# Second feed-forward GEMM of a transformer block by one level of Strassen, two u tiles at a time

## The chip, the cores and the metric

One core of a Trainium2 chip. The metric is the device time of one execution in microseconds (us). Two times are told apart by this kernel's measurement where they differ by over 0.2%.

## What is computed

The reference is a residual block on x of 1024 rows (tokens) by 1024 columns, all float32: a combined projection, two attentions, gates and an output projection, and then the feed-forward part, the only one that is touched here:

```python
h2 = rms_norm(x, g_mlp[l])
x = x + jnp.square(jax.nn.relu(h2 @ w_ff1[l])) @ w_ff2[l]
```

with w_ff1 of 1024 x 4096 and w_ff2 of 4096 x 1024. Below, u is the squared relu, kept transposed: 32 tiles of 128 of its 4096 columns, each 128 partitions x 1024 tokens.

## The kernel before

**Numbers.** Every float32 operand is split into a high part, rounded to fp32r by a copy, and a low part, the difference (`split` L794 on POOL for weights, line L796 for the high and L798 for the low part; ACT and DVE for activations). A product is three matmuls: high by high, high by low, low by high (`split_products` L1267, whose one line L1273 issues all of these matmuls). A matmul has 128 x 128 stationary numbers and streams 512 columns.

**Stages.** Up to the feed-forward part (start to about 735 us) nothing is changed. There h2 stands transposed and split in mT_hi and mT_lo (also called h2T), and the residual x in xr, 8 tiles of 128 tokens x 1024.

**Feed-forward part.** It runs in FF_GROUPS = 8 groups of GROUP = 4 u tiles. For each u tile PE does 48 matmuls (`up_half` L1582: 8 contraction tiles, 3 passes, 2 halves of the tokens) into PSUM banks 0 to 3, two tiles taking turns. Behind the four tiles it does the second GEMM of the same group (`ff` L1602): for each of 8 token tiles 24 matmuls (4 u tiles, 3 passes, 2 halves of the output columns) that sum in PSUM banks 4 to 7, two token tiles taking turns. So a group is 192 + 192 matmuls. ACT (`ff_up` L1240) evacuates relu (L1247) and writes the square twice, once as float32 (L1254) and once rounded (L1261). DVE (`ff_vec` L1988) makes the low part (L1995) and adds each finished token tile to xr (L2001).

**What sets the order.** There is no scheduler: each engine has its own list of instructions, in the order of the code, and waits for counts of semaphores that others raise. POOL (`ff_splits` L972) splits a raw 128 x 1024 piece of weights for w1 or w2 at a time. SP (`ff_loads` L758) issues the loads of those pieces in a ring of two. The weights of the next group's first two tiles are split while PE is in the second GEMM or at its end. The stage in PE's list:

```python
for j in range(2 if first else 0, GROUP):
    pe.wait_ge(relu_ready, 8 * g + 2 * j - 2)
    up_half(g, j, (0, 1)).then_inc(up_done, 1)
for t in range(T):
```

Of the kernel before, what the change touches and what calls it, by code (L numbers as in the profile page):

```python
# [84 lines left out]
def build(nc, x, positions, g_mix, w_in, b_gate, g_qa, g_ka, sinks_a, g_cq, g_ckv,  # L85
# [6 lines left out]
    with ExitStack() as ctx:  # L92
# [269 lines left out]
        relu_ready = sem("relu_ready")
        relu_sq_ready = sem("relu_sq_ready")
        uT_hi_done = sem("uT_hi_done")
        uT_ready = sem("uT_ready")
# [183 lines left out]


# [6 lines left out]
        def _(sp):  # L557
# [200 lines left out]
            def ff_loads(g, first):  # L758
                def load(n, what, j, *split):
                    for s_, v in split:  # L760
                        sp.wait_ge(s_, v)
                    if what == 1:
                        src = w1_d[:, bass.ds(g * (GROUP * P) + j * P, P)].rearrange("(k p) n -> p k n", p=P)
                        dst = raw[n % 2][:, :].rearrange("p (k n) -> p k n", n=P)
                    else:
                        src = w2_d[bass.ds(g * (GROUP * P) + j * P, P), :]
                        dst = raw[n % 2][:, :]
                    sp.dma_start(dst, src).then_inc(raw_landed[n % 2], 16)
                load(0, 1, 0, (ow_ready, 7) if first else (w1_ready, 4 * g))
                load(1, 1, 1, (ow_ready, 8) if first else (w2_ready, 4 * g))  # L770
                load(2, 2, 0, (w1_ready, 4 * g + 1))
                load(3, 2, 1, (w1_ready, 4 * g + 2))
                load(4, 1, 2, (w2_ready, 4 * g + 1))
                load(5, 2, 2, (w2_ready, 4 * g + 2))
                load(6, 1, 3, (w1_ready, 4 * g + 3))
                load(7, 2, 3, (w2_ready, 4 * g + 3))
# [8 lines left out]
        def _(pool):  # L785
# [186 lines left out]
            def ff_splits(g, first):  # L972
                landed = 16 * 4 + 64 * g

                def unit(n, what, j):
                    pool.wait_ge(raw_landed[n % 2], landed + 16 * (n // 2 + 1))
                    if what == 1:
                        if first and j < 2:
                            pool.wait_ge(branch_done, 2 * KD)
                        else:  # L980
                            pool.wait_ge(up_done, 4 * g + j - 1)
                        split(raw[n % 2][:, :].rearrange("p (k n) -> p k n", n=P), w1_hi[j % 2][:, :, :],
                              w1_lo[j % 2][:, :, :], w1_hi_done, 4 * g + j + 1, w1_ready)
                    else:
                        if j == 0:
                            if first:
                                pool.wait_ge(x2T_done, 2 * KD)
                            else:
                                pool.wait_ge(down_done, T * g)
                        split(raw[n % 2][:, :], w2_hi[j][:, :], w2_lo[j][:, :], w2_hi_done, 4 * g + j + 1, w2_ready)  # L990
                unit(0, 1, 0)
                if first:
                    for t in range(T):
                        pool.wait_ge(x2_ms_ready, t + 1)
                        power(x_rstd[:, t:t + 1], x_ms[:, t:t + 1], 1, (P, 1)).then_inc(x2_rstd_ready, 1)
                unit(1, 1, 1)
                unit(2, 2, 0)
                unit(3, 2, 1)
                unit(4, 1, 2)
                unit(5, 2, 2)  # L1000
                unit(6, 1, 3)
                unit(7, 2, 3)
# [1021 lines left out]
```

## Time and profile before

| | |
|---|---|
| median of 3 runs | 1444.29 us (1444.26 to 1444.85) |
| the profiled execution, its own time | 1444.09 us |
| its span, first to last instruction | 1442.3 us |
| feed-forward part, first matmul to end of span | 734.85 to 1442.3 us |
| PE, DVE, ACT, POOL busy over the span | 98%, 37%, 26%, 36% |

The profile is of one execution. PE is the matmul engine, DVE the vector engine, ACT the activation engine, POOL the general one, SP the one that issues DMAs. Matmuls are pipelined, so that the busy time of one (389 ns) is longer than the distance from the start of one to the start of the next. In rows of the timeline "x24" means that many merged, and what stands in brackets is the idle time before them and who ended it.

### The profile page before, as it was taken

The page shows a single profiled execution, that of the slowest core. Times are in us where ns is not written, and L with a number is a line of the kernel's source. Part 1 is how long each engine was busy: PE and PEld are TensorE (multiplying, and loading weights), DVE is VectorE, ACT ScalarE, POOL GpSimd, SP SyncE. Part 2 cuts the span into 40 slices and gives each one's busy share as a digit, 9 for nine tenths or more (in the row PEclk, how much of TensorE's full clock was granted, in tenths as well). Part 3 has the DMA queues.
Part 4 walks back from the last instruction along what each step waited for, and adds up shares of the span by engine and source line. Part 5 has one row for each costly group of instructions (what it writes and reads, how often), then busy time and mean ns, then how long its engine had stood idle before and what let it go on. Part 6 is the DMA issues. An engine that isn't in the chain of part 4 may idle for free.

```text
span 1442.3 us, 17282 instructions
## 1 busy us (share of the span) xinstructions
PE 1409.5 (98%) x6792; PEld 1154.7 (80%) x6792; DVE 533.2 (37%) x947; ACT 367.8 (26%) x811; POOL 525.0 (36%) x381
## 2 busy tenths in 40 slices
PE   6999999999999999999999999999999999999998
PEld 6998776778877667888888888888888888888887
DVE  5402714533668762472443222222222213222222
ACT  5113235642456552010232020110301102021020
POOL 2332823436382610454045060431506125061420
PEclk9999999999999999999999999999999999999999
DMA  7120221211120015535012030110202102020102
GB/s 234 35 59 31 72 88 59 67 57 42 39 47 12 12 16 129 186 132 182 0 44 88 0 103 15 59 58 18 84 15 73 44 29 87 0 87 29 44 29 102
DMA packets 98105, 90.45 MB, mean 63 GB/s; under 512 B 21376, under 2 KB 84352, under 8 KB 98048
## 3 DMA queue, kind: packets, MB, share of 16 engines
q1 hardware_dynamic: 97904, 89.17, 20.4%
q8 instruction: 36, 0.59, 0.2%
q10 hardware_dynamic: 144, 0.52, 0.1%
q14 instruction: 21, 0.17, 0.0%
HBM read 76.99 MB, written 12.62 MB: 62 GB/s over the span
## 4 chain that ended last, share of the span: by engine, by line
PE 87%; DVE 5%; POOL 2%; ACT 2%; issue 2%; DMA 1%; ACTq 0%; DVEq 0%; SPq 0%; POOLq 0%
PE PS L1273 75%; PE PS L1467 3%; PE PS L1280 2%; PE PS L1366 1%; PE PS L1417 1%; DVE uT_lo L1995 1%; PE PS L1447 1%; PE PS L1388 1%; PE PS L1448 1%; PE PS L1368 1%; PE PS L1449 1%; PE PS L1431 1%; PE PS L1403 1%; ACT gate L1073 1%; POOL scA L914 0%
## 5 line engine op out<-in xcount | busy, mean ns | idle before, releaser
L796 POOL TENSOR_SCALAR w_hi<-raw 128x1024 fp32r<-128x1024 f32 x64 | 74.3, 1160 | 408.2 <-PE PS L1273 406.7
L1995 DVE TENSOR_TENSOR uT_lo<-relu_sq,uT_hi 128x512 fp32r<-128x512 f32 x64 | 92.0, 1472 | 279.0 <-ACT uT_hi L1261 279.0
L1247 ACT ACTIVATE relu_t<-PS 128x512 f32<-128x512 f32 x64 | 34.8, 595 | 553.3 <-PE PS L1273 553.3
L2001 DVE TENSOR_TENSOR xr<-PS,xr 128x1024 f32<-128x1024 f32 x64 | 78.4, 1224 | 245.7 <-PE PS L1273 245.7
L798 POOL TENSOR_TENSOR w_lo<-raw,w_hi 128x1024 fp32r<-128x1024 f32 x64 | 159.4, 2491 | 5.3
L1273 PE MATMUL PS<-mT_hi,w_hi 128*128 128x512 f32 x512 | 160.4, 389 | 0.7 <-POOL w_lo L798 0.7
L1273 PE MATMUL PS<-mT_hi,w_lo 128*128 128x512 f32 x512 | 160.3, 389 | 0.0
L1273 PE MATMUL PS<-mT_lo,w_hi 128*128 128x512 f32 x512 | 160.2, 389 | 0.0
L1273 PE MATMUL PS<-w_hi,uT_hi 128*128 128x512 f32 x512 | 158.4, 391 | 1.7 <-DVE uT_lo L1995 1.7
L1273 PE MATMUL PS<-w_lo,uT_hi 128*128 128x512 f32 x512 | 157.7, 389 | 0.0
L1273 PE MATMUL PS<-w_hi,uT_lo 128*128 128x512 f32 x512 | 157.7, 389 | 0.0
L1273 PEld LDWEIGHTS PS<-w_hi,uT_hi 128*128 128x128 f32 x512 | 95.6, 188 | 24.1 <-DVE uT_lo L1995 3.9
L1273 PEld LDWEIGHTS PS<-mT_hi,w_hi 128*128 128x128 f32 x512 | 96.1, 188 | 20.8 <-issue 0.9
L1273 PEld LDWEIGHTS PS<-w_hi,uT_lo 128*128 128x128 f32 x512 | 96.1, 188 | 20.0
L1273 PEld LDWEIGHTS PS<-w_lo,uT_hi 128*128 128x128 f32 x512 | 96.1, 188 | 20.0
L1273 PEld LDWEIGHTS PS<-mT_hi,w_lo 128*128 128x128 f32 x512 | 96.1, 188 | 20.0
L1273 PEld LDWEIGHTS PS<-mT_lo,w_hi 128*128 128x128 f32 x512 | 96.1, 188 | 19.9
L1273 PE MATMUL PS<-hT_hi,gw_hi 128*128 128x512 f32 x256 | 84.7, 412 | 5.0 <-ACT gate L1073 2.6
L1273 PE MATMUL PS<-hT_lo,gw_hi 128*128 128x512 f32 x256 | 79.4, 391 | 0.0
L1273 PE MATMUL PS<-hT_hi,gw_lo 128*128 128x512 f32 x256 | 79.2, 390 | 0.0
L1273 PE MATMUL PS<-zw_hi,hT_hi 128*128 128x320 f32 (+1 forms) x256 | 77.7, 303 | 0.0
L1273 PE MATMUL PS<-zw_hi,hT_lo 128*128 128x320 f32 (+1 forms) x256 | 77.0, 301 | 0.0
(208 smaller groups left out, 2390.0 us busy)
## 6 DMA issues: line engine op xcount, KB each, us to landing
raw<-in_w_ff SPq DMA_DIRECT2D x64, 512.0 KB, 3.7
g_raw<-in_w_in SPq DMA_DIRECT2D x16, 512.0 KB, 3.9
gate_store<-gate SPq DMA_DIRECT2D x16, 512.0 KB, 2.6
x_in<-in_x SPq DMA_DIRECT2D x8, 512.0 KB, 10.7
gate_a<-gate_store SPq DMA_DIRECT2D x8, 512.0 KB, 7.7
gate_b<-gate_store SPq DMA_DIRECT2D x8, 512.0 KB, 5.6
raw<-in_w_out SPq DMA_DIRECT2D x8, 512.0 KB, 3.6
xr<-in_x SPq DMA_DIRECT2D x8, 512.0 KB, 7.0
```

The costliest lines, as they stand in the source:

```text
L796: pool.tensor_scalar(hi_ap, raw_ap, 1.0, 1.0, ALU.mult, ALU.mult).then_inc(hi_done, 1)
L798: pool.tensor_tensor(lo_ap, raw_ap, hi_ap, ALU.subtract).then_inc(ready, 1)
L1073: act.activation(gate[u % 2][:, :], pair(gate_pair(u)), ACT.Sigmoid, bias=b_gate_c[:, u:u + 1]).then_inc(gate_ready, 1)
L1247: act.activation(relu_t[:, cols], PS[:, 2 * (j % 2) + h, :], ACT.Relu).then_inc(relu_ready, 1)
L1273: ins = pe.matmul(o, st, cut(mv), start=first and n == 0, stop=last and n == 2)
L1280: ins = pe.transpose(PS[0:rows, bank, i * P:(i + 1) * P], ap, ident[:, :])
L1366: pe.matmul(PS[:, bank, 0:B_GROUP * QK], cqT[:, c, rows], wuq[g % 2][:, c, :], start=c == 0, stop=c == 1)
L1368: pe.matmul(PS[:, bank, B_GROUP * QK:B_GROUP * (QK + P)], ckvT[:, rows], wukv[g % 2][:, :], start=True, stop=True).then_inc(proj_done, 1)
L1388: ins = pe.matmul(PS[:, 2 * s + g % 2, 256 * (g // 2):256 * (g // 2) + WIN], qaT[r:r + A_DIM, head // 2, m * P:(m + 1) * P], kaT[r:r + A_D ...
L1467: ins = pe.matmul(out[:, c0:HALF], vB[g % 3][:, kt, h % B_GROUP, :], p_tile(t)[:, c0:HALF], start=kt == 0, stop=last)
L1995: dve.tensor_tensor(uT_lo[:, j, cols], relu_sq[:, cols], uT_hi[:, j, cols], ALU.subtract).then_inc(uT_ready, 1)
L2001: dve.tensor_tensor(xr[:, t, :], pair(4 + 2 * (t % 2)), xr[:, t, :], ALU.add).then_inc(x3_added, 1)
```

## The change

The u tiles are taken in 16 pairs: pair i holds the tiles i and i + 16. The 2 x 2 blocks of a pair's product are: 512 tokens by one u tile on one side, one u tile by 512 output columns on the other. One level of Strassen (in Winograd's form) takes 7 products of such blocks instead of 8, out of sums and differences of the blocks. For a pair, PE does 7 products x 4 token tiles x 3 passes = 84 matmuls, each product into its own sum: four of them lie in the quarters of xr, three in sum1, sum6 and sum7 in SBUF. A product's token tile is 3 matmuls in one PSUM bank and is added to its sum at once by DVE. The last pair is done plainly (96 matmuls), while the running sums are folded into one another. The first GEMM keeps its 96 matmuls for a pair.

What the engines do for one pair i of the first 15: PE, `up` of pair i + 1 (2 tiles of 48 matmuls), then `down` of pair i (28 steps of 3). POOL: two splits of w1 (128 x 1024), 4 differences of w2 blocks and 7 splits of 128 x 512. ACT: 15 operations of 128 x 512. DVE: 4 sums and 7 low parts of 128 x 512, and 28 additions of a PSUM bank into a sum. A raw weight block is loaded into the place where later its low part stands (w2_raw, w1_raw), so that a load waits until PE has done with what was there. The loops of the stage are written out, in place of loops that run on the chip.

```diff
-GROUP = 4
-FF_GROUPS = D_FF // P // GROUP
+PAIRS = D_FF // P // 2
+BLOCKS7 = 28
+LAST = PAIRS - 1
...
-        uT_hi = place("uT_hi", 72, [P, GROUP, S], F32R)
-        uT_lo = place("uT_lo", 88, [P, GROUP, S], F32R)
-        relu_t = place("relu_t", 197, [P, S])
-        relu_sq = place("relu_sq", 201, [P, S])
+        w1_hi = [place(f"w1_hi{i}", 136 + 8 * i, [P, KD, P], F32R) for i in range(2)]
+        w1_lo = [place(f"w1_lo{i}", 140 + 8 * i, [P, KD, P], F32R) for i in range(2)]
+        w2_hi = [place(f"w2_hi{b}", 72 + 4 * b, [P, HALF], F32R) for b in range(7)]
+        w2_lo = [place(f"w2_lo{b}", 74 + 4 * b, [P, HALF], F32R) for b in range(7)]
+        u_hi = [place(f"u_hi{b}", 100 + 4 * b, [P, HALF], F32R) for b in range(7)]
+        u_lo = [place(f"u_lo{b}", 102 + 4 * b, [P, HALF], F32R) for b in range(7)]
...
+        sum1 = place("sum1", 128, [P, 4, HALF])
+        sum6 = place("sum6", 153, [P, 4, HALF])
+        sum7 = place("sum7", 193, [P, 4, HALF])
+        relu_t = place("relu_t", 201, [P, HALF])
+        r11 = place("r11", 203, [P, HALF])
+        r12 = place("r12", 205, [P, HALF])
...
+        PRODUCTS = (1, 2, 3, 5, 7, 6, 4)
+        AT = {p: b for b, p in enumerate(PRODUCTS)}
...
+        def wait_used(eng, i, p):
+            if i:
+                eng.wait_ge(down_done, BLOCKS7 * (i - 1) + 4 * AT[p] + 4)
+        def acc(p):
+            if p in (1, 6, 7):
+                return {1: sum1, 6: sum6, 7: sum7}[p][:, :, :]
+            rows, cols = {2: (0, 0), 3: (0, 1), 4: (1, 0), 5: (1, 1)}[p]
+            return xr[:, 4 * rows:4 * rows + 4, HALF * cols:HALF * cols + HALF]
...
+            def w1_load(i, j):
+                if i:
+                    sp.wait_ge(up_done, 2 * i - 1 + j)
+                f = i + PAIRS * j
+                sp.dma_start(w1_raw[j][:, :, :], w1_d[:, f * P:(f + 1) * P].rearrange("(k p) n -> p k n", p=P)
+                             ).then_inc(w1_landed[j], 16)
+            def w2_load(i, n):
+                p, row, col = ((1, 0, 0), (2, 1, 0), (3, 1, 1), (5, 0, 1))[n]
+                if i == 0:
+                    sp.wait_ge(o_done, 2 * T)
+                wait_used(sp, i, p)
+                f = i + PAIRS * row
+                sp.dma_start(w2_raw[AT[p]][:, :], w2_d[f * P:(f + 1) * P, HALF * col:HALF * col + HALF]
+                             ).then_inc(w2_landed[n], 16)
...
+            w1_load(1, 0)
+            for i in range(1, PAIRS):
+                w1_load(i, 1)
+                for n in range(3):
+                    w2_load(i, n)
+                if i + 1 < PAIRS:
+                    w1_load(i + 1, 0)
+                w2_load(i, 3)
...
+            def w1_split(i, j):
+                pool.wait_ge(w1_landed[j], 16 * (i + 1))
+                split(w1_raw[j][:, :, :], w1_hi[j][:, :, :], w1_lo[j][:, :, :], w1_hi_done, 2 * i + j + 1, w1_ready)
...
+            def w2_difference(out, a, b):
+                pool.tensor_tensor(w2_raw[AT[out]][:, :], w2_raw[AT[a]][:, :], w2_raw[AT[b]][:, :], ALU.subtract
+                                   ).then_inc(w2_step, 1)
+            def w2_first(i):
+                for n in range(4):
+                    if n != 1:
+                        pool.wait_ge(w2_landed[n], 16 * (i + 1))
+                wait_used(pool, i, 7)
+                w2_difference(7, 3, 5)
+                pool.wait_ge(w2_step, w2_count(i, "t3"))
+                w2_difference(5, 5, 1)
+                w2_high(AT[1])
+                w2_low(i, AT[1], "b11_hi")
+                wait_used(pool, i, 6)
+                w2_difference(6, 3, 5)
+                w2_high(AT[3])
+                w2_low(i, AT[3], "b22_hi")
+                w2_high(AT[5])
+                w2_low(i, AT[5], "t1_hi")
+            def w2_second(i):
+                pool.wait_ge(w2_landed[1], 16 * (i + 1))
+                wait_used(pool, i, 4)
+                if i == 0:
+                    pool.wait_ge(x2T_done, 2 * KD)
+                w2_difference(4, 2, 6)
+                w2_high(AT[2])
+                w2_low(i, AT[2], "b21_hi")
+                w2_high(AT[7])
+                w2_low(i, AT[7], "t3_hi")
+                w2_high(AT[6])
+                w2_low(i, AT[6], "t2_hi")
+                w2_high(AT[4])
+                w2_low(i, AT[4], "t4_hi")
...
+            def fold(into, p, blocks):
+                pool.wait_ge(acc_done, BLOCKS7 * (LAST - 1) + blocks)
+                pool.tensor_tensor(acc(into), acc(into), acc(p), ALU.add).then_inc(folded, 1)
+            w1_split(0, 0)
+            w1_split(0, 1)
+            for t in range(T):
+                pool.wait_ge(x2_ms_ready, t + 1)
+                power(x_rstd[:, t:t + 1], x_ms[:, t:t + 1], 1, (P, 1)).then_inc(x2_rstd_ready, 1)
+            w2_first(0)
+            w1_split(1, 0)
+            for i in range(LAST):
+                w2_second(i)
+                w1_split(i + 1, 1)
+                if i + 2 < PAIRS:
+                    w1_split(i + 2, 0)
+                if i + 1 < LAST:
+                    w2_first(i + 1)
+            fold(6, 1, 4)
+            fold(2, 1, 8)
+            w2_plain(0, 1, "b11_hi")
+            w2_plain(1, 2, "b21_hi")
+            w2_plain(2, 3, "b22_hi")
+            fold(3, 5, 16)
+            w2_plain(3, 5, "b12_hi")
+            pool.wait_ge(folded, 3)
+            fold(3, 6, 24)
...
+            def up(i, c):
+                j, k = c // KD, c % KD
+                if k == 0:
+                    pe.wait_ge(w1_ready, 2 * i + j + 1)
+                    pe.wait_ge(u_act, act_count(i - 1, ("relu21", "relu22")[j]))
+                ins = up_chunk(j, k, (0, 1))
+                if k == KD - 1:
+                    ins.then_inc(up_done, 1)
+            def down(d, n):
+                b, q = n // 4, n % 4
+                p, rows = PRODUCTS[b], slice(q * P, (q + 1) * P)
+                if q == 0:
+                    pe.wait_ge(u_vec, vec_count(d, U_OF[p]))
+                    pe.wait_ge(w2_step, w2_count(d, W_OF[p]))
+                if BLOCKS7 * d + n >= 4:
+                    pe.wait_ge(acc_done, BLOCKS7 * d + n - 3)
+                split_products(u_hi[b][:, rows], u_lo[b][:, rows], w2_hi[b][:, :], w2_lo[b][:, :],
+                               [(PS[:, 4 + q, :], whole)], 0, True, True).then_inc(down_done, 1)
...
+            for d in range(LAST):
+                for c in range(2 * KD):
+                    up(d + 1, c)
+                for n in range(BLOCKS7):
+                    down(d, n)
+            for t, k in ((0, 0), (1, 0), (0, 1), (1, 1)):
+                plain(t, k)
+            for t in range(2, T):
+                for k in range(2):
+                    plain(t, k)
...
+            def accumulate(d, n):
+                p, q = PRODUCTS[n // 4], n % 4
+                dve.wait_ge(down_done, BLOCKS7 * d + n + 1)
+                if q == 0 and d:
+                    dve.wait_ge(acc_done, BLOCKS7 * (d - 1) + n + 4)
+                if d == LAST - 1 and n == 4 * AT[6]:
+                    dve.wait_ge(folded, 1)
+                out, part = acc(p)[:, q, :], PS[:, 4 + q, :]
+                if d == 0 and p in (1, 6, 7):
+                    dve.tensor_copy(out, part).then_inc(acc_done, 1)
+                else:
+                    dve.tensor_tensor(out, part, out, ALU.add).then_inc(acc_done, 1)
...
+            def combine(d):
+                low(d, 2, r12[:, :], "hi12")
+                s2(d)
+                s4(d)
+                s1(d)
+                sum_low(d, 3, "s4_hi")
+                sum_low(d, 5, "s1_hi")
+                sum_low(d, 7, "s3_hi")
+                sum_low(d, 6, "s2_hi")
+                sum_low(d, 4, "hi22")
...
+            for d in range(LAST):
+                combine(d)
+                for n in range(BLOCKS7):
+                    accumulate(d, n)
+                low(d + 1, 1, r11[:, :], "hi11")
+                if d + 1 < LAST:
+                    s3(d + 1)
+                else:
+                    sum_low(LAST, 5, "hi21")
...
```

In the parts that are left out, `w2_high` and `w2_low` are the two halves of `split` for a block of w2, `act_count`, `vec_count` and `w2_count` give a step's number in the lists of ACT, DVE and POOL, `combine` and the ACT steps name blocks by 11, 12, 21, 22 (token half, u tile of the pair), and `plain` is the last pair.

POOL, the steps of one pair in the middle of the stage. Before, two tiles of w1 and then w2 pieces in turn, with one wait for PE at the start (w1_hi0 needs up_done), here from the first split of a group:

```order
L796 TENSOR_SCALAR w1_hi0<-raw0 128x1024 [waits up_done,raw_landed0]
L798 TENSOR_TENSOR w1_lo0<-raw0,w1_hi0 128x1024 [waits w1_hi_done]
L796 TENSOR_SCALAR w1_hi1<-raw1 128x1024 [waits up_done,raw_landed1]
L798 TENSOR_TENSOR w1_lo1<-raw1,w1_hi1 128x1024 [waits w1_hi_done]
L796 TENSOR_SCALAR w2_hi0<-raw0 128x1024 [waits down_done,raw_landed0]
L798 TENSOR_TENSOR w2_lo0<-raw0,w2_hi0 128x1024 [waits w2_hi_done]
```

Before, w1 of a group's first tiles comes ahead of its w2. Now, from `w1_split(i + 2, 0)` on (number behind w2_ is the block's place in PRODUCTS):

```order
L851 TENSOR_SCALAR w1_hi0<-w1_raw0 128x1024 [waits w1_landed0]
L853 TENSOR_TENSOR w1_lo0<-w1_raw0,w1_hi0 128x1024 [waits w1_hi_done]
L1039 TENSOR_TENSOR w2_raw4<-w2_raw2,w2_raw3 128x512 [waits w2_landed3,down_done,w2_landed2,w2_landed0]
L1039 TENSOR_TENSOR w2_raw3<-w2_raw3,w2_raw0 128x512 [waits w2_step]
L1032 TENSOR_SCALAR w2_hi0<-w2_raw0 128x512
L1036 TENSOR_TENSOR w2_lo0<-w2_raw0,w2_hi0 128x512 [waits w2_step]
L1039 TENSOR_TENSOR w2_raw5<-w2_raw2,w2_raw3 128x512 [waits down_done]
L1032 TENSOR_SCALAR w2_hi2<-w2_raw2 128x512
L1036 TENSOR_TENSOR w2_lo2<-w2_raw2,w2_hi2 128x512 [waits w2_step]
L1032 TENSOR_SCALAR w2_hi3<-w2_raw3 128x512
L1036 TENSOR_TENSOR w2_lo3<-w2_raw3,w2_hi3 128x512 [waits w2_step]
```

and right behind these rows `w2_second` of the same pair and `w1_split(i + 1, 1)`:

```order
L1039 TENSOR_TENSOR w2_raw6<-w2_raw1,w2_raw5 128x512 [waits down_done,w2_landed1]
L1032 TENSOR_SCALAR w2_hi1<-w2_raw1 128x512
L1036 TENSOR_TENSOR w2_lo1<-w2_raw1,w2_hi1 128x512 [waits w2_step]
L1032 TENSOR_SCALAR w2_hi4<-w2_raw4 128x512
L1036 TENSOR_TENSOR w2_lo4<-w2_raw4,w2_hi4 128x512 [waits w2_step]
L1032 TENSOR_SCALAR w2_hi5<-w2_raw5 128x512
L1036 TENSOR_TENSOR w2_lo5<-w2_raw5,w2_hi5 128x512 [waits w2_step]
L1032 TENSOR_SCALAR w2_hi6<-w2_raw6 128x512
L1036 TENSOR_TENSOR w2_lo6<-w2_raw6,w2_hi6 128x512 [waits w2_step]
L851 TENSOR_SCALAR w1_hi1<-w1_raw1 128x1024 [waits w1_landed1]
L853 TENSOR_TENSOR w1_lo1<-w1_raw1,w1_hi1 128x1024 [waits w1_hi_done]
```

The second tile of w1 (w1_hi1, w1_lo1) now stands behind all 18 steps on w2, and of those the ones from w2_raw6 on wait for the end of `down` of the pair before. In PE's list a `down` ends and the next `up` begins so:

```order
L1413 MATMUL PS<-w2_hi6,u_hi6 128x512 [waits acc_done]
L1413 MATMUL PS<-w2_lo6,u_hi6 128x512
L1413 MATMUL PS<-w2_hi6,u_lo6 128x512
L1413 MATMUL PS<-mT_hi,w1_hi0 128x512 [waits u_act,w1_ready]
L1413 MATMUL PS<-mT_hi,w1_hi0 128x512
L1413 MATMUL PS<-mT_lo,w1_hi0 128x512 x2
```

Each of the 28 steps waits for the addition of four steps before (acc_done), and each of the two `up` tiles waits for its w1 (w1_ready); the second one stands 48 matmuls behind the first.

## Rows read from the trace of the kernel before

**Rows 1.** Page, busy time by engine, whole span.
```profile
PE 1409.5 (98%) x6792; PEld 1154.7 (80%) x6792; DVE 533.2 (37%) x947; ACT 367.8 (26%) x811; POOL 525.0 (36%) x381
```
**Rows 2.** Waits from 735 us on: who for whom, total us, times, longest us.
```profile
PE PS L1273 <- DVE uT_lo L1995: 1.7, 7, 0.3
```
**Rows 3.** Chain that ended last, in order of time: start, us, what.
```profile
743.02 38.38 PE PS L1273 x168
...
871.31 2.00 DVE uT_lo L1995
873.35 83.28 PE PS L1273 x366
958.87 2.00 DVE uT_lo L1995
...
1438.00 1.22 DVE xr L2001
```
**Rows 4.** Timeline of DVE, second GEMM: start, us, engine, line.
```profile
880.49 1.22 DVE L2001 TENSOR_TENSOR xr<-PS,xr 128x1024 f32<-128x1024 f32 x1 [4.22 <-PE PS L1273]
885.93 1.22 DVE L2001 TENSOR_TENSOR xr<-PS,xr 128x1024 f32<-128x1024 f32 x1 [4.22 <-PE PS L1273]
```
**Rows 5.** Issues of DMAs: KB each, us from issue to landing.
```profile
raw<-in_w_ff SPq DMA_DIRECT2D x64, 512.0 KB, 3.7
```
**Rows 6.** Timeline of POOL, splits of 128 x 1024.
```profile
913.25 1.05 POOL L796 TENSOR_SCALAR w_hi<-raw 128x1024 fp32r<-128x1024 f32 x1 [40.51 <-PE PS L1273]
914.39 2.39 POOL L798 TENSOR_TENSOR w_lo<-raw,w_hi 128x1024 fp32r<-128x1024 f32 x1
916.75 1.05 POOL L796 TENSOR_SCALAR w_hi<-raw 128x1024 fp32r<-128x1024 f32 x1
...
927.63 1.49 POOL L796 TENSOR_SCALAR w_hi<-raw 128x1024 fp32r<-128x1024 f32 x1
929.21 2.71 POOL L798 TENSOR_TENSOR w_lo<-raw,w_hi 128x1024 fp32r<-128x1024 f32 x1
```
**Rows 7.** Timeline of POOL, splits of 128 x 512 in the branch stage.
```profile
573.11 0.62 POOL L796 TENSOR_SCALAR bw_hi<-b_raw 128x512 fp32r<-128x512 f32 x1 [62.00 <-DMA b_raw<-in_w_branch_b]
573.81 1.30 POOL L798 TENSOR_TENSOR bw_lo<-b_raw,bw_hi 128x512 fp32r<-128x512 f32 x1
575.16 0.62 POOL L796 TENSOR_SCALAR bw_hi<-b_raw 128x512 fp32r<-128x512 f32 x1
```
**Rows 8.** Timeline of DVE beside the splits of rows 6.
```profile
926.32 3.35 DVE L1995 TENSOR_TENSOR uT_lo<-relu_sq,uT_hi 128x512 fp32r<-128x512 f32 x2 [11.96 <-ACT uT_hi L1261]
```
**Rows 9.** Timeline of DVE, merge of the branches, beside the splits of rows 10.
```profile
628.95 3.42 DVE L1940 TENSOR_TENSOR mT_lo<-gate_b,mT_hi 128x1024 fp32r<-128x1024 f32 x1
632.29 1.21 DVE L1933 TENSOR_TENSOR gate_b<-PS,gate_b 128x1024 f32<-128x1024 f32 x1
```
**Rows 10.** Timeline of POOL in the same stretch.
```profile
628.04 3.25 POOL L798 TENSOR_TENSOR ow_lo<-raw,ow_hi 128x1024 fp32r<-128x1024 f32 x1
631.24 2.04 POOL L796 TENSOR_SCALAR ow_hi<-raw 128x1024 fp32r<-128x1024 f32 x1
```
**Rows 11.** Timeline of DVE: four reads of a PSUM bank in a row.
```profile
741.69 2.48 DVE L1957 TENSOR_TENSOR mT_lo<-PS,mT_hi 128x512 fp32r<-128x512 f32 x4 [1.04 <-ACT mT_hi L1229]
```
**Rows 12.** Timeline of PE, start of the kernel.
```profile
9.86 1.94 PE L1280 MATMUL PS<-ident,x_in 128*128 128x128 f32 x8 [9.86 <-DVE x_in L1633]
...
17.62 0.47 PE L1273 MATMUL PS<-zw_lo,hT_hi 128*128 128x320 f32 x1
17.88 0.47 PE L1273 MATMUL PS<-zw_hi,hT_lo 128*128 128x320 f32 x1
...
19.09 0.31 PE L1273 MATMUL PS<-zw_hi,hT_hi 128*128 128x320 f32 x1
19.24 0.31 PE L1273 MATMUL PS<-zw_lo,hT_hi 128*128 128x320 f32 x1
```
**Rows 13.** Windows: length, busy us by engine, granted TensorE clock, DMA share, GB/s.
```profile
14.00:18.00 4.00, 4.00 (x18) 4.00 (x17) 3.34 (x5) 2.74 (x6) 0.55 (x1) 1.00 1.01 403
```

More of the change, by code:

```diff
@@ L358, in build @@
         w1_ready = sem("w1_ready")
-        w2_hi_done = sem("w2_hi_done")
-        w2_ready = sem("w2_ready")
+        w1_landed = [sem(f"w1_landed{i}") for i in range(2)]
+        w2_landed = [sem(f"w2_landed{i}") for i in range(4)]
+        w2_step = sem("w2_step")
         up_done = sem("up_done")
[L362 to L365, printed above, removed]
+        u_act = sem("u_act")
+        u_vec = sem("u_vec")
         down_done = sem("down_done")
+        acc_done = sem("acc_done")
+        folded = sem("folded")
         x3_added = sem("x3_added")
@@ L755, in _ @@
                 out_load(k)
[L758 to L776, printed above, removed]
@@ L777, in _ @@
-            peeled(sp, FF_GROUPS, ff_loads)
+            def w1_load(i, j):
[12 more added lines that the diff above has]
+                             ).then_inc(w2_landed[n], 16)
@@ L969, in _ @@
                 split(raw[k % 2][:, :], ow_hi[k][:, :], ow_lo[k][:, :], ow_hi_done, k + 1, ow_ready)
[L972 to L1002, printed above, removed]
@@ L1262, in _, with relu, square, sum_high @@
-            peeled(act, FF_GROUPS, ff_up)
+            def relu(i, tile, half, before):
+                act.wait_ge(up_done, 2 * i + tile + 1)
+                if before is not None:
+                    act.wait_ge(u_act, act_count(*before))
+                act.activation(relu_t[:, :], PS[:, 2 * tile + half, :], ACT.Relu).then_inc(u_act, 1)
+            def square(out):
+                act.activation(out, relu_t[:, :], ACT.Square).then_inc(u_act, 1)
+            def sum_high(i, p, step):
+                act.wait_ge(u_vec, vec_count(i, step))
+                wait_used(act, i, p)
+                act.activation(u_hi[AT[p]][:, :], u_raw[AT[p]][:, :], ACT.Copy).then_inc(u_act, 1)
@@ L1265, in _ @@
+            for i in range(PAIRS):
+                first_tile(i)
+                second_tile(i)
         @block.tensor
@@ new lines, in whole, with plain @@
+            def whole(v):
+                return v
+            def plain(t, k):
+                half, rows = t // 4, slice((t % 4) * P, (t % 4 + 1) * P)
+                u = AT[((1, 2), (5, 4))[half][k]]
+                if t in (0, 4):
+                    pe.wait_ge(u_vec, vec_count(LAST, (("lo11", "lo12"), ("lo21", "lo22"))[half][k]))
+                if t == 0:
+                    pe.wait_ge(w2_step, w2_count(LAST, "b12_lo"))
+                if k == 0:
+                    if t < 2:
+                        pe.wait_ge(acc_done, BLOCKS7 * LAST - 2 + 2 * t)
+                    else:
+                        pe.wait_ge(x3_added, t - 1)
+                w = ((1, 5), (2, 3))[k]
+                passes = ((u_hi, w2_hi), (u_hi, w2_lo), (u_lo, w2_hi))
+                for m, (st, mv) in enumerate(passes):
+                    for col in range(2):
+                        ins = pe.matmul(PS[:, 4 + 2 * (t % 2) + col, :], st[u][:, rows], mv[AT[w[col]]][:, :],
+                                        start=k == 0 and m == 0, stop=k == 1 and m == 2)
+                if k:
+                    ins.then_inc(down_done, 1)
@@ new lines, in _ @@
+            dve.wait_ge(acc_done, BLOCKS7 * LAST)
+            link(dve, dve.tensor_tensor(acc(7), acc(7), acc(6), ALU.add))
+            sum_low(LAST, 4, "hi22")
+            for t in range(T):
+                dve.wait_ge(down_done, BLOCKS7 * LAST + t + 1)
+                if t == 0:
+                    dve.wait_ge(folded, 4)
+                dve.tensor_tensor(xr[:, t, :], pair(4 + 2 * (t % 2)), xr[:, t, :], ALU.add).then_inc(x3_added, 1)
+                if t == 0:
+                    link(dve, dve.tensor_tensor(acc(5), acc(5), acc(7), ALU.add))
+                if t == 1:
+                    link(dve, dve.tensor_tensor(acc(4), acc(4), acc(7), ALU.add))
```

187 lines of the change are left out of this document (109 added, 78 removed).

## The prediction

> **What bounds the kernel now.** Read the busy times first: PE is busy for 98% of the span, the next engine for 37% [rows 1]. The waits of the feed-forward part show whom PE waits for: in seven groups 1.7 us in all, for DVE's low part [rows 2]. Then the chain: it is PE, in stretches of 366 matmuls of 83.28 us, with one DVE piece between them, and it repeats every 958.87 - 871.31 = 87.56 us [rows 3]. That is a group of 384 matmuls, so 0.228 us each, with 0.5 us left over. The clean distance is in the second GEMM: 24 matmuls between two additions of DVE, 885.93 - 880.49 = 5.44 us, so 0.2267 us each [rows 4]. PE sets the pace, at one matmul per 0.2267 us, and two u tiles (a pair) cost 43.8 us.
>
> **What the change removes from PE.** The first GEMM stays at 96 matmuls a pair. The second has 84 instead of 96 in 15 pairs: 180 matmuls fewer, 40.8 us. If PE still set the pace, a pair would last 180 x 0.2267 = 40.8 us, of which 21.8 are `up` (10.9 for each tile) and 19.04 `down` (0.68 for a step of three). The question is who else must be ready in that time. The additions of DVE can: four reads of a PSUM bank take 2.48 us in a row, 0.62 each [rows 11], under the 0.68 of a step, and they don't suffer from POOL (1,024 columns out of PSUM took 1.21 us beside a split of POOL [rows 9], against 1.22 alone [rows 4]). I cost them at nothing. PE's many waits for them I cost at nothing too, since the bank was freed three steps before.
>
> **POOL's chain.** POOL's work on a pair is not long, but its order makes a loop with PE. Let S be the start of `down` of pair d and T = S + 19.0 its end; at T PE goes on with `up` of pair d + 2, whose two tiles wait for their splits of w1. The second of these splits is the end of this chain:
>
> 1. In SP's list the load of w1's first tile of pair d + 2 stands behind the load of the third w2 block of pair d + 1, which waits for 12 steps of `down`: 12 x 0.68 = 8.2 us.
> 2. It lands 3.7 us later [rows 5]. S + 11.9.
> 3. POOL splits it; PE needs this tile at T and has it: 913.25 to 916.75, 3.5 us [rows 6]. S + 15.4. (`w2_first` could start at S + 13.6, at step 20; the order puts it behind this split.)
> 4. `w2_first` of pair d + 1: three differences and three splits of 128 x 512. A split of that size with what follows it lasts 575.16 - 573.11 = 2.05 us [rows 7], next ones 2.0; I take 2.0. A difference is a two-operand operation like the low part, 1.30 us there. 3 x 2.0 + 3 x 1.3 = 9.9 us. S + 25.3.
> 5. `w2_second`: one difference, four splits, 9.3 us. S + 34.6. It waits for the end of `down`, S + 19.0, which is past by then.
> 6. `w1_split` of the second tile, 3.5 us. S + 38.1, and 0.2 for the semaphore.
> 7. Beside all of this DVE makes the sums and low parts of u, 11 operations whose operands are both in SBUF. Beside two such POOL's operations took 1.49 and 2.71 us in place of 1.05 and 2.39 [rows 6, 8]: 0.76 us, 0.38 for one. 11 x 0.38 = 4.2 us. S + 42.5.
> 8. PE has ended the first tile of `up` at T + 10.9 = S + 29.9 and stands still for 12.6 us. Then the second tile, 10.9 us, and the next `down` begins at S + 53.4.
> 9. After so long a stop PE may begin slowly. At the start of the kernel it had been idle for 9.86 us and its matmuls of 320 columns then stood 0.267 us apart, from 14.80 to about 18.15, and 0.147 later [rows 12]: the levels of 1.2 and 2.4 GHz. That cost 1.5 us on the matmuls from 14.80, 2.5 us if counted from 13.18, where PE resumed for good. I take 2.0.
>
> The Trainium skill (TensorE: Matmul & The Clock Gate, section "Why this matters for your kernels") tells to avoid idle gaps between bursts of matmuls since the clock falls to half in them. By it the penalty comes after every stop; the row on the granted clock says 1.00 for that same stretch at the start [rows 13], and by that row alone it would be nothing. The distances at the start agree with the page and not with that column. The 2.0 above stands on those distances.
>
> So a pair lasts 55.4 us in place of 43.8. The change doesn't take 3 us off each pair, it adds 11.6.
>
> **DVE and ACT in this loop.** DVE's 11 operations last 1.68 us each beside POOL (3.35 for two [rows 8]): 18.5 us, with about 3 us of waiting for ACT in between, since ACT's s3_hi waits for a sum that DVE makes behind its 28 additions. They end about T + 22.5; `down` needs them at T + 34, when it begins. They are covered by PE's stop. Without that stop `down` would begin at T + 21.8, could do four steps before it needs the first addition, and would have no slack left: DVE is the next bound.
>
> **The ends.** The first pair's `up` ends at 743.02 + 72 x 0.2267 = 759.3 (behind the transposes, as before) [rows 3]. The load of pair 1's first w1 tile waits for 48 of these, 753.9, lands 757.6, is split by 761.1. Behind it come `w2_second` and a split of w1, 9.3 + 3.5 + 4.2, 778.1. PE's second tile ends at 789.0, and with 1 us for a slow clock the first `down` starts at 790. The 15th starts 14 x 55.4 = 775.6 later, 1565.6. Behind the last pair's split POOL has in order: two folds of 128 x 2048 (2 x 2.39 = 4.8 us each [rows 6], the first from S + 3.5), three splits (6.0), a fold (4.8), a split (2.0), and about 1 us lost to DVE, so that the plain pair starts at S + 27 and not at S + 19. Its 96 matmuls take 21.8 us, 1.5 more for waits on the folded sums, 2.0 for the clock; the last addition 1.2, the store 3.1 (from 1439.2 to 1442.3 before) [rows 3]. S + 56.6. The span ends at 1622. Around the span lie 1444.09 - 1442.3 = 1.8 us. The profiled execution is 0.2 us under the median, so nothing is added for that. **1624 us.**
>
> **Bounds of the unknown costs.** The loss to DVE: below 0 (DVE beside POOL loses nothing where it reads PSUM [rows 9]), above 0.93 for an operation (0.86 + 0.99 us beside one of twice the size [rows 9, 10]), 10.2 us a pair. I take 4.2, the row with this size of operand. The clock: 0 to 2.5 a pair. The landing: 3.7, and up to 5 since 256 and 512 KB start together. Each microsecond in the loop counts 14 times. All low: 49.2 us a pair, 1530 us. Landing, clock and half of the possible loss high: 60 us, 1690.
>
> **Rivals.**
> - *PE sets the pace after all* (ends on the other side). Then 759.3 + 15 x 40.8 + 21.8 + 1.2 + 3.1 = 1397.4, and 1.8: 1399 us, 45 faster. It needs POOL's chain, from the 12th step of `down` to the second w1 split, to end within 16 x 0.68 + 10.9 = 21.8 us. It adds to 30.1 with no loss to DVE at all [rows 5 to 7]. It decides for "faster" at 42.7 us a pair, (1442.3 - 790 - 55) / 14, a chain of 23.6 us: POOL's operations would have to be a quarter shorter than their rows [rows 6, 7], and those repeat to the hundredth. For it speaks only that POOL's whole work (26 us a pair) fits into a pair. 3 in 100; no change, 1 in 100, is a point between.
> - *POOL sets the pace but loses nothing to DVE and the clock holds*: 49.2 us a pair, 1530 to 1560 us. For it: the granted clock of 1.00 in all rows. Against it: the losses and the distances at the start [rows 6, 8, 12]. 7 in 100.
> - *The clock stays at 1.2 GHz for the whole second tile*, 48 matmuls at 512 / 1.2 = 0.427 us, 20.5 us in place of 10.9: 7.6 us a pair beyond my 2.0, 1730 us. Against it: at the start it rose within 5 us of steady work [rows 12]. Or the loss to DVE is near its upper bound, 1700. 7 in 100 for both.
> - *The change doesn't do what it says*, PE having as many matmuls as before: the order shows 28 steps of 3 a pair. Not counted.
>
> **How the numbers follow.** My forecast, POOL's loop with both losses, has 82 in 100, at 1624 us. The range that holds the time 8 times in 10 leaves out the rival below 1560 and the one above 1680. Faster by over 0.2% 0.03, within 0.2% 0.01, slower by over 0.2% 0.96; 0.2% is about what a measurement of this kernel can tell.
>
> **What would show it.** PE's waits: 14 waits for POOL's w_lo of 12 to 13 us each, at the ninth contraction of `up`, always the second tile; none in `down`. The chain: POOL's w2 splits and differences for about half of the stage, PE's share near 85%. POOL busy nearly without a gap from S + 12 to S + 42 and then idle for some 20 us. A period of 55 us between the starts of `down`. Matmuls 0.43 us apart behind each stop, and 0.2267 after that. DVE's 512-column subtractions near 1.7 us, its additions near 0.62. Wrong would be: PE waiting in `down` (then DVE's sums are late), or a w1 split that ends before PE needs it.

## The result, and the profile after

The changed kernel took 1637.86 us (median of 4 runs, 1637.03 to 1639.25), the kernel before 1444.46 us beside it. The ratio is 1.1339, with a 95% interval of 1.132 to 1.1359: 13% slower. Forecast were 1624 us, in a range of 1560 to 1680. The profiled execution took 1637.03 us, of which its span is 1634.9.

The page of the changed kernel, busy time by engine (first row; the answer to [rows 1]), the shares of the chain that ended last by engine, and the issues of w1 and w2 blocks (KB each, us to landing; the answer to [rows 5]):

```profile
PE 1404.8 (86%) x6612; PEld 1143.5 (70%) x6612; DVE 892.6 (55%) x1420; ACT 405.5 (25%) x856; POOL 765.9 (47%) x599
...
PE 61%; POOL 26%; DVE 4%; DMA 4%; issue 3%; ACT 1%; SPq 0%; DVEq 0%; POOLq 0%; ACTq 0%
...
w_raw<-in_w_ff SPq DMA_DIRECT2D x32, 512.0 KB, 4.3
w_raw<-in_w_ff SPq DMA_DIRECT2D x64, 256.0 KB, 2.6
```

PE has its 180 matmuls fewer, 6612 in place of 6792. Yet its busy time is only 4.7 us less than in [rows 1], not 40.8: the matmuls that are left took longer. POOL is busy for 47% of the time and holds 26% of the chain. An engine can bound a kernel while it is idle for half of it.

The waits of the changed kernel from 735 us on (who for whom, us in total, times, longest us), where [rows 2] had 1.7 us:

```profile
POOL w_hi L851 <- DMA w_raw<-in_w_ff: 372.0, 15, 27.5
...
PE PS L1413 <- POOL w_lo L853: 190.3, 16, 13.8
...
PE PS L1777 <- issue: 6.9, 1, 6.9
```

PE waits for POOL's low part of w1, as forecast. And POOL itself waits, up to 27.5 us at a time, for a load of w1, which SP issues only when PE has done 12 steps of `down`. Each engine waits for the other in turn, so this is a closed loop; too much work on POOL would not leave it idle for so long.

The chain that ended last, in order of time, one turn of that loop (start, us, what; the answer to [rows 3]):

```profile
999.89 20.71 PE PS L1413 x84
...
1020.61 0.33 SPq L818
...
1020.99 4.11 DMA w_raw<-in_w_ff
...
1025.18 1.05 POOL w_hi L851
...
1050.67 1.26 POOL w_lo L1036
1051.94 1.02 POOL w_hi L851
1053.03 2.35 POOL w_lo L853
1055.42 21.90 PE PS L1413 x84
```

The 84 matmuls are the 48 of the second w1 tile and the first 12 steps of `down`; then SP issues, the block lands, and POOL works for 30.2 us before PE goes on. The first second tile begins at 775.60 and the fifteenth at 1563.85, so a pair lasts 788.25 / 14 = 56.3 us, against 43.8 before. POOL's timeline shows what the 30.2 us hold (start, us, operation; compare [rows 7]):

```profile
1032.00 1.29 POOL L1036 TENSOR_TENSOR w_lo<-w_raw,w_hi 128x512 fp32r<-128x512 f32 x1
1033.25 1.74 POOL L1039 TENSOR_TENSOR w_raw<-w_raw 128x512 f32<-128x512 f32 x1
1034.96 1.06 POOL L1032 TENSOR_SCALAR w_hi<-w_raw 128x512 fp32r<-128x512 f32 x1
...
1042.62 1.58 POOL L1036 TENSOR_TENSOR w_lo<-w_raw,w_hi 128x512 fp32r<-128x512 f32 x1
```

DVE in the same stretch, its five last low parts:

```profile
1043.00 7.12 DVE L2180 TENSOR_TENSOR u_lo<-u_raw,u_hi 128x512 fp32r<-128x512 f32 x5
```

Beside DVE's sums and low parts a POOL operation takes 0.3 to 0.45 us more than the 1.29 and 0.61 alone. And PE, timeline and windows behind the stop (windows: length, busy us of PE, PEld, DVE, ACT, POOL, granted clock, DMA share, GB/s):

```profile
1055.42 1.22 PE L1413 MATMUL PS<-mT_hi,w_hi 128*128 128x512 f32 x2 [13.08 <-POOL w_lo L853]
1056.44 1.05 PE L1413 MATMUL PS<-mT_lo,w_hi 128*128 128x512 f32 x2
1057.29 1.05 PE L1413 MATMUL PS<-mT_hi,w_lo 128*128 128x512 f32 x2
```

```profile
1055.40:1059.00 3.60, 3.58 (x8) 2.81 (x9) 0.00 (x0) 0.00 (x0) 0.00 (x0) 0.50 0.00 0
...
1062.00:1066.00 4.00, 4.00 (x19) 3.31 (x18) 0.00 (x0) 0.00 (x0) 0.00 (x0) 1.00 0.00 0
```

Two matmuls begin every 0.85 us, 0.43 apart, at a granted clock of 0.50 (1.2 GHz), and from about 1061 on at 1.00 (2.4 GHz). The second tile takes 13.57 us here in place of 10.9, 2.7 us more. Behind the 14 long stops this loss is 1.5 to 3.0 us, 2.3 in the mean. The very first second tile lost nothing, though PE had stood for 3.23 us:

```profile
775.60 0.73 PE L1413 MATMUL PS<-mT_hi,w_hi 128*128 128x512 f32 x2 [3.23 <-POOL w_lo L853]
```

**Where the 193 us come from.** If PE had set the pace the span would end at 1397.4. Beyond that: 14 pairs of 56.3 in place of 40.8 us, 217 us; the first pair's waits, 5.5 (its `down` starts at 786.61 and not at 759.3 + 21.8); a slower clock in the last turn than in the first, 2.6; and the end, 57.4 us behind the last `down`'s start (1577.47) in place of 45.1, 12.3. Together 237.5 us, of which the 44.9 come off by which such a span would be shorter than the 1442.3 before: 192.6 between the two profiled spans. Of the 15.5 us in a pair, 13.2 are the stop and 2.3 the clock.

### The profile page after: what moved, and what is told of

It reads as the page before. It is cut to its first block, busy times and chain, and to the rows that moved or that the text cites. A ratio compares the mean times of both kernels' runs of the same rounds, so it can differ in the third digit from the quotient of the medians.

```text
span 1634.9 us, 17512 instructions
## 1 busy us (share of the span) xinstructions
PE 1404.8 (86%) x6612; PEld 1143.5 (70%) x6612; DVE 892.6 (55%) x1420; ACT 405.5 (25%) x856; POOL 765.9 (47%) x599
## 4 chain that ended last, share of the span: by engine, by line
PE 61%; POOL 26%; DVE 4%; DMA 4%; issue 3%; ACT 1%; SPq 0%; DVEq 0%; POOLq 0%; ACTq 0%
PE PS L1413 48%; POOL w_lo L1036 9%; POOL w_hi L1032 5%; POOL w_raw L1039 5%; DMA w_raw<-in_w_ff 3%; PE PS L1607 3%; POOL w_lo L853 3%; PE PS L1420 2%; POOL w_hi L851 2%; PE PS L1777 1%; PE PS L1506 1%; PE PS L1557 1%; PE PS L1587 1%; PE PS L1528 1%; PE PS L1588 1%
## 5 line engine op out<-in xcount | busy, mean ns | idle before, releaser
L2176 DVE TENSOR_TENSOR sum<-PS,sum 128x512 f32<-128x512 f32 x168 | 114.6, 692 | 284.3 <-PE PS L1413 284.3
L1036 POOL TENSOR_TENSOR w_lo<-w_raw,w_hi 128x512 fp32r<-128x512 f32 x109 | 162.8, 1493 | 9.1
L2176 DVE TENSOR_TENSOR xr<-PS,xr 128x512 f32<-128x512 f32 x240 | 163.6, 692 | 0.0
L1413 PE MATMUL PS<-w_hi,u_hi 128*128 128x512 f32 x420 | 163.4, 389 | 0.0
L1413 PE MATMUL PS<-w_lo,u_hi 128*128 128x512 f32 x420 | 163.4, 389 | 0.0
L1413 PE MATMUL PS<-w_hi,u_lo 128*128 128x512 f32 x420 | 163.4, 389 | 0.0
L2180 DVE TENSOR_TENSOR u_lo<-u_raw,u_hi 128x512 fp32r<-128x512 f32 x77 | 102.1, 1386 | 0.0
L1032 POOL TENSOR_SCALAR w_hi<-w_raw 128x512 fp32r<-128x512 f32 x109 | 96.3, 883 | 0.0
L1039 POOL TENSOR_TENSOR w_raw<-w_raw 128x512 f32<-128x512 f32 x60 | 92.3, 1538 | 3.2 <-DMA w_raw<-in_w_ff 2.0
L1413 PEld LDWEIGHTS PS<-w_hi,u_lo 128*128 128x128 f32 x420 | 78.9, 188 | 16.4
```

Source lines behind the costliest of these rows:

```text
L1032: pool.tensor_scalar(w2_hi[b][:, :], w2_raw[b][:, :], 1.0, 1.0, ALU.mult, ALU.mult).then_inc(w2_step, 1)
L1036: pool.tensor_tensor(w2_lo[b][:, :], w2_raw[b][:, :], w2_hi[b][:, :], ALU.subtract).then_inc(w2_step, 1)
L1039: pool.tensor_tensor(w2_raw[AT[out]][:, :], w2_raw[AT[a]][:, :], w2_raw[AT[b]][:, :], ALU.subtract).then_inc(w2_step, 1)
L1413: ins = pe.matmul(o, st, cut(mv), start=first and n == 0, stop=last and n == 2)
L2176: dve.tensor_tensor(out, part, out, ALU.add).then_inc(acc_done, 1)
L2180: dve.tensor_tensor(u_lo[AT[p]][:, :], raw_ap, u_hi[AT[p]][:, :], ALU.subtract).then_inc(u_vec, 1)
```

## The experiments

The theory T: POOL's order closes a loop with PE, and everything between the landing of w1's first tile and the split of its second counts in full. The rivals: POOL's or DVE's load is what bounds (L), so that an order would move little; or the granted clock (K). e3, e4, e5, e7 and e8 were run once each; repeated runs of the others lie up to 5.7 us apart.

**e1, only POOL's order.** The second w1 split moves ahead of `w2_second`; the same instructions.

```diff
             for i in range(LAST):
-                w2_second(i)
                 w1_split(i + 1, 1)
+                w2_second(i)
```

> One line moved in POOL's list: the second w1 split of a pair stands ahead of w2_second instead of behind it. Theory A (the order of POOL's list closes a loop with PE; the stop before the second tile is only that): the split is then there about 9 + 4 us earlier plus the later half of the loss to DVE, and of the 13 us stop 0 to 3 us remain, so a pair lasts 41 to 44 us and the kernel 1425 to 1460 us. Theory B (POOL and DVE together have too much work for a pair, so the order matters little): the stop moves to another place, into down, and the time stays over 1550 us.

Measured: 1464.65 us (1461.8 to 1467.51), 1.015 of the kernel before [1.0124, 1.0175]. 173 us came off with not one instruction less, though 5 us fewer than I had expected at least. L falls. What is left can be seen in e1's waits, PE's timeline and windows (columns as above):

```profile
PE PS L1413 <- POOL w_lo L853: 34.0, 15, 3.2
```

```profile
945.16 0.73 PE L1413 MATMUL PS<-mT_hi,w_hi 128*128 128x512 f32 x2 [3.13 <-POOL w_lo L853]
...
1032.81 1.22 PE L1413 MATMUL PS<-mT_hi,w_hi 128*128 128x512 f32 x2 [3.20 <-POOL w_lo L853]
```

```profile
1025.00:1029.00 4.00, 4.00 (x20) 3.30 (x19) 3.96 (x3) 1.05 (x2) 3.92 (x4) 1.00 0.01 2
1032.80:1038.00 5.20, 5.19 (x12) 4.13 (x13) 4.89 (x4) 0.00 (x0) 5.12 (x4) 0.50 0.01 3
1038.90:1045.00 6.10, 6.10 (x28) 5.03 (x27) 0.00 (x0) 0.00 (x0) 4.37 (x5) 1.00 0.00 0
```

Fifteen stops of 2.3 us in the mean, since the chain from the landing through `w2_first` still ends too late. Behind the stop of 3.20 us the granted clock is halved as behind one of 13: 12 matmuls in 5.2 us and not in 2.7. Behind the one of 3.13 us it is not. Of the fifteen, eight cost 1.1 to 2.7 us more for the clock (read from the first 24 matmuls behind each, against 0.2267 us a matmul) and seven at most 0.2, 1.0 in the mean. So a short stop costs here nearly one and a half times its length, and its length alone doesn't tell whether the clock falls.

**e2, SP's order and POOL's.** The second w1 tile is loaded and split one pair earlier, and the w2 loads stand behind both w1 loads.

```diff
+            w1_load(1, 1)
...
-                w1_load(i, 1)
-                for n in range(3):
-                    w2_load(i, n)
...
-                w2_load(i, 3)
+                    w1_load(i + 1, 1)
+                for n in range(4):
+                    w2_load(i, n)
...
+            w1_split(1, 1)
...
-                w1_split(i + 1, 1)
...
+                    w1_split(i + 2, 1)
```

> SP loads both w1 tiles of pair d + 2 ahead of the w2 blocks of pair d + 1, and POOL splits both ahead of w2_first. Theory A: no stop is left in the middle of the stage, a pair lasts 41 to 42 us, and what remains against 1399 us is the two ends and a small lateness of DVE: 1415 to 1435 us, faster than before the change. Theory B: over 1500 us, PE waiting in down for w2 splits or for DVE's sums.

Measured: 1414.18 us (1411.05 to 1414.5), 0.9793 of the kernel before [0.9776, 0.9809]: 2.1% faster than before, 224 us faster than the change, and 1 us below my expectation. Its waits, its chain in order of time, and a window of 400 us:

```profile
PE PS L1778 <- issue: 6.9, 1, 6.9
PE PS L1414 <- POOL w_lo L853: 2.3, 1, 2.3
```

```profile
752.52 4.07 DMA w_raw<-in_w_ff
...
760.20 611.89 PE PS L1414 x2691
...
1396.93 11.17 PE PS L1778 x48
```

```profile
900.00:1300.00 400.00, 400.00 (x1766) 331.24 (x1765) 327.11 (x385) 84.74 (x145) 285.64 (x215) 1.00 0.18 52
```

2691 matmuls follow each other for 611.89 us, 0.2274 us each. DVE is busy for 82% of the window and POOL for 71%, and PE waits for neither. The rival "PE sets the pace" had 1371.3 us for the end of the last `down`, 759.3 + 15 x 40.8; it ends at 1372.1. All but 1 of the 15 us by which e2 misses 1399 lie in the last, plain pair.

**e3 and e7, a dose of POOL work.** Four more rounding copies of 128 x 512 in `w2_second`, in the change's order (e3) and in e2's (e7).

```diff
+            def again(b):
+                doses[0] += 1
+                pool.tensor_scalar(w2_hi[b][:, :], w2_raw[b][:, :], 1.0, 1.0, ALU.mult, ALU.mult).then_inc(dose, 1)
+                pool.wait_ge(dose, doses[0])
...
+                again(AT[2])
...
```

> The change with four more rounding copies of 128 x 512 on POOL in w2_second (each written twice, the same numbers). Theory A: every POOL instruction between the third w2 load and the second w1 split counts in full, 4 x (0.6 to 1.05) us a pair, 15 pairs: 40 to 65 us more, 1675 to 1705 us. Rival C (the stop is set by the landing of the loads or by DVE, and POOL only looks late): within 10 us of 1638.

> The order of e2 with the four more rounding copies of e3. Theory A: POOL's list has slack there, since w2_second is due only in down, 3 to 4 us behind where it ends: 1410 to 1425 us, where the same four cost 37 us in the old order. If POOL's amount of work counts in any order: about 1450 us.

Measured: e3 1675.41 us, 37.5 more than the change, 2.5 us in each of 15 pairs for the four copies; e7 1414.06 us, where e2 has 1414.18. The same 2.5 us a pair cost everything in the one order and nothing in the other. e3 adds less than my 40 to 65, since a copy costs little beyond its undisturbed 0.62 us: where one takes 1.05 beside DVE, the kernel's own copies behind it are shorter, 0.93 and 0.62 us where they took 1.05 in the change's turn above, as POOL's timeline in e3 shows (L1065 is the added copy, L1033 one of the change's own):

```profile
1056.86 1.05 POOL L1065 TENSOR_SCALAR w_hi<-w_raw 128x512 fp32r<-128x512 f32 x1
1057.99 0.93 POOL L1033 TENSOR_SCALAR w_hi<-w_raw 128x512 fp32r<-128x512 f32 x1
...
1064.25 0.61 POOL L1065 TENSOR_SCALAR w_hi<-w_raw 128x512 fp32r<-128x512 f32 x1
1064.95 0.62 POOL L1033 TENSOR_SCALAR w_hi<-w_raw 128x512 fp32r<-128x512 f32 x1
```

**e8, only SP's order.** The first three pieces of e2's diff, with POOL's order as in the change.

> Only SP's list is changed: both w1 tiles are loaded as soon as their place is free, POOL's list is that of the change. Then the chain no longer starts with the 12th step, 4.2 us of landing and a split (S + 16.3) but with the 20th step (S + 13.6): 2.7 us a pair, 38 us less, 1595 to 1605 us, and the stop still there, about 10 us. If the landing of the loads were the main cause: under 1550 us.

Measured: 1599.90 us, 38 less. The landing and the first w1 split leave the loop, and `w2_first` is released by PE's steps and no longer by a load, but the two w2 groups still stand ahead of the second split: PE's waits for it are 150.7 us in e8, 10.4 a stop.

**e4, PE kept at work in the stop.** 48 matmuls of no use into a PSUM bank that is free by then, ahead of the second tile, from the third pair on.

```diff
+                if c == KD and i > 1:
+                    pe.wait_ge(acc_done, BLOCKS7 * (i - 1))
+                    for _ in range(48):
+                        pe.matmul(PS[:, 4, :], h2T_hi[:, 0, 0:P], h2T_hi[:, 1, 0:HALF], start=True, stop=True)
```

> The change with 48 matmuls of no use put into the stop ahead of the second tile of up (10.9 us of the 13 us), so that PE isn't idle long. Theory A with a price of 2 to 3 us a stop for the lower clock: 14 x 2 to 14 x 3 us less, 1597 to 1611 us, and the matmuls behind the stop 0.2267 us apart. If the clock cost nothing beyond what overlaps: 1638 us. If the added matmuls are in the way: above 1638.

Measured: 1613.37 us, 24.5 less, with more matmuls than the change. PE's timeline and a window behind one stop in e4:

```profile
1050.76 0.73 PE L1413 MATMUL PS<-mT_hi,w_hi 128*128 128x512 f32 x2 [2.32 <-POOL w_lo L853]
```

```profile
1050.80:1054.00 3.20, 3.20 (x14) 2.64 (x15) 0.00 (x0) 0.00 (x0) 0.00 (x0) 1.00 0.00 0
```

The real stop is 2.3 us and the clock 1.00: 14 matmuls in 3.2 us. The clock is a part of the cost, 1.75 us a stop by this run and 2.3 by the matmuls' distances, and K falls as the cause. I had expected 27 at least. Of the 8 us between 14 x 2.3 and 24.5, 4 can be seen: the first second tile, which has no added matmuls, came 1.0 us later than in the change and lost 1.7 to the clock, and one later stop (at 1159.55) lost 1.5 in spite of the added ones. The rest stays open.

**e5, no low parts on DVE.** `sum_low` writes zeros in the Strassen pairs, so that 5 of DVE's 11 operations don't read two operands in SBUF.

```diff
-                low(i, p, u_raw[AT[p]][:, :], high)
+                if i == LAST:
+                    low(i, p, u_raw[AT[p]][:, :], high)
+                    return
+                dve.wait_ge(u_act, act_count(i, high))
+                dve.memset(u_lo[AT[p]][:, :].bitcast(F32), 0.0).then_inc(u_vec, 1)
```

> The change with the low parts of the five u blocks that are sums (or u22) left out for the first 15 pairs: DVE writes zeros there, with the same waits, in place of a subtraction of two SBUF operands. POOL's list is untouched. If DVE's operations with two SBUF operands are what slows POOL (0.38 us each in the prediction, 4.0 us a pair for 11 in the trace of the change), 5 x 0.38 x 14 = 27 us less, 1605 to 1615 us, and POOL's operations beside the zeros at their undisturbed 0.62 and 1.29 us. If POOL is slow for a reason of its own: 1638 us.

Measured: 1608.22 us, 29.6 less, 2.0 in each of 15 pairs or 0.4 for each operation, near the 0.38 of the prediction's seventh step. POOL's timeline in e5, beside the zeros that DVE writes from 1033.06 to 1035.95:

```profile
1034.80 0.62 POOL L1032 TENSOR_SCALAR w_hi<-w_raw 128x512 fp32r<-128x512 f32 x1
1035.50 1.26 POOL L1036 TENSOR_TENSOR w_lo<-w_raw,w_hi 128x512 fp32r<-128x512 f32 x1
```

These writes cost POOL nothing, so what costs it time is DVE's operations that read two operands in SBUF.

**e6 and e9, the end of e2.** e6 is e2 with the plain pair's first split ahead of the second fold and its last ahead of the third. e9 is e6 with POOL's third fold held until DVE's last low part, and DVE's sum of two accumulators behind its first token tile.

```diff
+            w2_plain(0, 1, "b11_hi")
             fold(2, 1, 8)
-            w2_plain(0, 1, "b11_hi")
...
+            w2_plain(3, 5, "b12_hi")
             fold(3, 5, 16)
-            w2_plain(3, 5, "b12_hi")
```

and in e9 beyond that:

```diff
+            pool.wait_ge(u_vec, vec_count(LAST, "lo22"))
             fold(3, 5, 16)
...
+            sum_low(LAST, 4, "hi22")
             dve.wait_ge(acc_done, BLOCKS7 * LAST)
-            link(dve, dve.tensor_tensor(acc(7), acc(7), acc(6), ALU.add))
-            sum_low(LAST, 4, "hi22")
...
                 if t == 0:
+                    link(dve, dve.tensor_tensor(acc(7), acc(7), acc(6), ALU.add))
```

> The order of e2, and in the end the four plain splits of w2 ahead of the third fold. In e2 PE stands still for 6.9 us there and runs at the lower clock behind it. The plain pair then waits about 2 us in place of 6.9: 3 to 8 us less than e2, 1406 to 1411 us. If the folds (which PE's third token tile waits for) are the bound of the end and not the splits: as e2, 1414 us.

> e6 with the two long folds on POOL held back until DVE has made the last three low parts, and DVE's fold of sum6 into sum7 moved behind the first token tile. In e6 two of these low parts (0.69 us alone) last 5.05 and 4.97 us beside POOL's folds of 5.02 and 4.83, and PE waits 6.86 us for them. If that is the collision on operands in SBUF: the low parts back at about 0.7 us, the wait of 6.86 us gone, a later one of some us for the folds in its place, 1404 to 1410 us. If the folds' own length is the bound of the end: 1411 to 1415 us.

Measured: e6 1411.96 us, 0.9785 of the kernel before [0.9768, 0.9801]; e9 1413.58 us, 0.98 [0.9782, 0.9817]. The two and e2 can't be told apart. DVE and then POOL in e6, timeline:

```profile
1372.94 5.05 DVE L2181 TENSOR_TENSOR u_lo<-u_raw,u_hi 128x512 fp32r<-128x512 f32 x1
1377.92 4.97 DVE L2181 TENSOR_TENSOR u_lo<-r,u_hi 128x512 fp32r<-128x512 f32 x1
...
1385.13 0.69 DVE L2181 TENSOR_TENSOR u_lo<-u_raw,u_hi 128x512 fp32r<-128x512 f32 x1
...
1372.43 5.02 POOL L1083 TENSOR_TENSOR xr<-xr 128x2048 f32<-128x2048 f32 x1
1377.52 4.83 POOL L1083 TENSOR_TENSOR xr<-xr,sum 128x2048 f32<-128x2048 f32 x1
```

A low part of 0.69 us lasts 5 us because a fold of POOL runs, and ends 0.5 us behind that fold. e9 took that collision away (its low parts take 0.68 us), and DVE then waited 9.4 us for the folds, which follow later. PE's longest stop is 6.9 us in e6 and 6.7 in e9: the wait changed its name only. My 1406 to 1411 for e6 was missed by 1 us and my 1404 to 1410 for e9 by 3.6. Other divisions of the folds were not tried, so the end stays open by up to some 13 us.

## Why the prediction was right

**POOL's loop.** Right, and shown: the same instructions in another order take the time from 1637.9 to 1414.2 (e2), and a dose counts in full in the one order and not at all in the other (e3, e7).

**Steps 1 to 6.** The steps of `down` and POOL's undisturbed durations came as in their rows. Step 2, the landing, was mis-sized: 4.1 us and more, and 0.3 to issue, in place of 3.7. The page's median of 4.3 us for 512 KB against [rows 5] is the same finding. The loads of w1 and w2 are now issued right behind each other, but no run separates that as the reason. The 0.2 for a semaphore stood on no row; the chain has 0.04 us there.

**Step 7, the loss to DVE.** From the first split at 1025.18 to PE at 1055.42 are 30.2 us; the rows without DVE give 26.2. So 4.0 was lost where the prediction had 4.2, and e5 gave 0.4 for an operation where it had 0.38. The row of the same operand size was the right one to take.

**Steps 8 and 9, stop and clock.** The 14 stops are 13.1 to 13.8 us, 13.2 in the mean for 12.6, at the ninth contraction, always in the second tile. The clock took 2.3 us in the mean (1.5 to 3.0, from the start of the second tile to the next `down`, less 10.9) in place of 2.0. The Trainium skill (TensorE: Matmul & The Clock Gate, section "Why this matters for your kernels") was right here for the long stops, against the 1.00 of [rows 13]: matmuls stood 0.43 us apart behind all 14, at a granted clock of 0.50. The shorter ones went either way: PE's first, of 2.05 us, cost 1.7 us, and the next, of 3.23, nothing. The stop, longer by 0.6 us through the landing, and the clock, 0.3 more, make the 0.9 us by which a pair is longer than 55.4, and 14 x 0.9 = 12.6 us of the 13 that the span is over its forecast; the misses at the two ends cancel.

**DVE as the next bound.** This step failed. The prediction had DVE's 11 operations at 1.68 us and no slack without PE's stop. The lines of DVE in the changed kernel, 800 to 1540 us, by shape (busy us, mean ns, idle before):

```profile
L2176 DVE TENSOR_TENSOR xr<-PS,xr 128x512 f32<-128x512 f32 x212 | 144.5, 692 | 0.0
...
L2180 DVE TENSOR_TENSOR u_lo<-u_raw,u_hi 128x512 fp32r<-128x512 f32 x65 | 87.3, 1405 | 0.0
L2180 DVE TENSOR_TENSOR u_lo<-r,u_hi 128x512 fp32r<-128x512 f32 x26 | 27.4, 1054 | 31.6 <-ACT u_hi L1351 31.6
L2187 DVE TENSOR_TENSOR u_raw<-r,u_raw 128x512 f32<-128x512 f32 x13 | 22.4, 1723 | 0.0
```

Only three of the four sums take 1.6 to 1.7 us; the low parts, seven of the 11, take 1.05 to 1.4. DVE ended at T + 18.8 in the turn shown above (1050.1, where `down` ended at 1031.3) and not at T + 22.5. With no stop in 612 us (e2) PE never waited for it. The mistake was to price all 11 by a row of two. (The 692 ns of an addition are no contradiction to the 0.62 of [rows 11]: in `down` eight take 5.45 us in a row, 0.68 from one to the next, which is PE's step.)

**The ends.** The first second tile came at 775.60 for 778.1, PE's last stop was 6.9 us for 8, and the end S + 57.4 for S + 56.6.

**The rival of 1399 us** was refused since the chain adds to 30.1 us by rows alone; in the change it took 34.8 from issue to PE. It was no fault of Strassen's: with the order mended it came true to 1 us in the middle.

## What to carry to other kernels

Between engines with lists in fixed order, add up all that stands between the event that releases an engine and the item that the bottleneck needs, and compare it with the time the bottleneck can go on meanwhile; the engine's total load, 26 us of a 41 us pair here, doesn't decide it. Put what the bottleneck needs next at the front of the list, and its load a round ahead, before judging an algorithm that saves work by its first timing. Where the order is right a helper engine can be 82% busy at no cost.
